# A decoder trunk on eight cores: the first weight block in four transfers with products tile by tile, and retention in chunks of 128 with seven f32 accumulators

## What is computed

```python
q = rotary(rq, pos); k = rotary(rk, pos) * RET_DK**-0.5; v = rv      # 4 heads, 256 wide
def step(S, blk):                                                     # retention, in chunks of C tokens
    s = einsum('bihd,bjhd->bhij', qc, kc) * inner                     # decay mask inside the chunk
    o = einsum('bhij,bjhe->bihe', s, vc) + einsum('bihd,bhde->bihe', qc, S) * q_dec
    S = S * chunk_dec + einsum('bjhd,bjhe->bhde', kc * k_dec, vc)
    return S, o
o = o * rsqrt(mean(o*o) + EPS) * ret_norm_g;  y_ret = (o * silu(rg)) @ w_ret_o
pre = cc * cu;  conv = conv_b + sum(conv_w[t] * xp[:, t:t+L] for t in range(3))
y_conv = (cb * conv * silu(cg)) @ w_conv_o
om = softmax(qm mem_k^T) mem_v * silu(mg);  y_mem = om @ w_mem_o
y = x + (g_ret*y_ret + g_conv*y_conv + g_mem*y_mem) @ w_out;  out = rms_norm(y, final_norm_g)
```

## Time and profile before

| | |
|---|---|
| median of 3 runs | 1253.17 us (1251.75 to 1255.77) |
| the profiled execution | 1262.68 us; its slowest core, core 1, has a span of 1261.1 us |
| spans of the eight cores | 1238.0 to 1261.1 us |
| mean granted TensorE clock | 0.972 to 0.978 on cores 0 to 3, 0.987 to 0.993 on cores 4 to 7 |
| TensorE busy, core 1 | 1190.1 us (94%), 7140 products |
| VectorE, ScalarE, POOL busy | 585.2 us (46%), 461.1 us (37%), 332.6 us (26%) |

### The profile page before, as it was taken

The page is one execution under the profiler, slowest core; times in us unless marked ns, Lnnn a source line. Parts: engine busy times, 40 slices in busy tenths (PEclk is TensorE's granted clock), DMA queues, the critical chain, the costliest instruction groups (busy, mean ns, idle before and its releaser), DMA issues.

```text
span 1261.1 us, 22033 instructions; the slowest of 8 cores (1238.0 to 1261.1 us)
## 1 busy us (share of the span) xinstructions
PE 1190.1 (94%) x7140; PEld 605.1 (48%) x7140; DVE 585.2 (46%) x1058; ACT 461.1 (37%) x1010; POOL 332.6 (26%) x424
## 2 busy tenths in 40 slices
PE   3889999999999999999999999989989799999997
PEld 1444444445554554554444544545545445444443
DVE  3764444442222355556212356556565565322266
ACT  3442233322222444444211254545445346322233
POOL 2332222221000111011333434435334344333300
PEclk9999999999999999999999999989999999999989
DMA  9734111112555686974421033724734633811074
GB/s 219 189 85 67 35 34 35 34 34 39 100 101 101 121 135 114 150 120 82 114 52 34 15 104 128 197 96 137 201 118 145 159 126 106 246 35 34 2 253 164
DMA packets 38000, 134.34 MB, mean 107 GB/s; under 512 B 4736, under 2 KB 8960, under 8 KB 33024
## 3 DMA queue, kind: packets, MB, share of 16 engines
q0 software_dynamic: 10080, 56.63, 27.0%
q1 hardware_dynamic: 27808, 76.30, 18.4%
HBM read 160.56 MB, written 28.98 MB: 150 GB/s over the span
## 4 chain that ended last, share of the span: by engine, by line
PE 75%; DVE 7%; DMA 6%; ACT 5%; issue 4%; SPq 1%; POOL 1%; DVEq 0%; ACTq 0%; POOLq 0%
PE psf L416 73%; DVE tf L1107 3%; DMA pms<-c_maskX 2%; DMA nrp<-arF 2%; DMA arF<-c_cos 1%; PE psh L419 1%; DMA mgd<-xp 1%; ACT th L944 1%; ACT ob L1238 1%; ACT arH L1304 1%; ACT mgd L476 1%; DVE th L953 1%; DVE mgd L485 0%; DVE ssb L940 0%; ACT arH L1164 0%
## 5 line engine op out<-in xcount | busy, mean ns | idle before, releaser
L416 PE MATMUL psf<-hT,w 128*128 128x512 bf16 (+1 forms) x3456 | 694.1, 355 | 3.1 <-ACT hT L499 1.5
L416 PEld LDWEIGHTS psf<-hT,w 128*128 128x128 bf16 x3456 | 315.7, 99 | 336.4 <-issue 44.9
L416 PE MATMUL psf<-ob,w 128*128 128x512 bf16 (+1 forms) x960 | 200.1, 352 | 0.0
L556 ACT ACTIVATE tf<-psf,hbg 128x512 f32<-128x512 f32 (+1 forms) x95 | 60.2, 633 | 210.7 <-PE psf L416 206.7
L416 PEld LDWEIGHTS psf<-ob,w 128*128 128x128 bf16 x960 | 87.8, 99 | 93.5 <-issue 12.0
L416 PE MATMUL psf<-w,hT 128*128 128x512 bf16 (+1 forms) x608 | 130.3, 368 | 1.1 <-ACT th L944 1.1
L567 DVE SCALAR_TENSOR_TENSOR tf<-tf,psf 128x512 f32<-128x512 f32 (+1 forms) x79 | 48.0, 607 | 176.2 <-PE psf L416 168.0
L571 POOL TENSOR_TENSOR mgd<-tf,mgd 128x512 bf16<-128x512 f32 (+1 forms) x79 | 78.8, 1005 | 160.1 <-DVE tf L567 160.1
L1107 DVE TENSOR_TENSOR tf<-psf,arF 128x512 f32<-128x512 f32 (+1 forms) x160 | 95.7, 610 | 29.0 <-POOL arH L1110 7.4
L416 PEld LDWEIGHTS psf<-w,hT 128*128 128x128 bf16 x608 | 59.3, 99 | 59.9 <-issue 6.1
L1110 POOL TENSOR_TENSOR th<-tf 128x512 bf16<-128x512 f32 x32 | 40.7, 1270 | 157.2 <-DVE tf L1107 122.2
(11 more groups left out here) (180 smaller groups left out, 1183.5 us busy)
## 6 DMA issues: line engine op xcount, KB each, us to landing
w<-wb POOLq DMA_DIRECT2D x38, 1024.0 KB, 10.8
mgd<-xp SPq DMA_DIRECT2D x16, 512.0 KB, 11.9
arH<-cmk POOLq DMA_DIRECT2D x12, 512.0 KB, 17.1
arH<-cmv POOLq DMA_DIRECT2D x10, 512.0 KB, 11.8
gaux<-sret SPq DMA_DIRECT2D x8, 512.0 KB, 4.4
xbuf<-sret SPq DMA_DIRECT2D x8, 512.0 KB, 5.1
stgt<-sret SPq DMA_DIRECT2D x8, 512.0 KB, 4.6
hbt<-sret SPq DMA_DIRECT2D x8, 512.0 KB, 5.7
```

The costliest lines, as they stand in the source:

```text
L416: P.op('pe', lambda e: e.matmul(out, lhsT=lhsT, rhs=rhs, start=start, stop=stop), reads=reads, writes=[wbuf])
L556: P.op('act', lambda e, fg=fg, ti=ti, n=n, bcol=bcol: e.activation(out=tf[ti][:, 0:n], in_=psf[fg][:, 0:n], func=AF.Tanh, bias=hbg[:, bcol ...
```

## The change

Four things change together.

1. Start. The first weight block comes in four transfers, one for each product group (the blocks 0 to 7 are packed so that a group's weights lie together), asked for in the order cu, cc, cb, cg from the moment the first token tile is there. Only four token tiles are asked for at first; the next four wait for the third tile's sum. `hT` and the weight slots are tracked in finer pieces. The cu products of group 0 and all four groups of token group 1 are done tile by tile (8 products of 128 columns for each). A dummy activation is put ahead on ScalarE.
2. Conv items. The order of the first items is (0,0), (0,1), (1,0), (1,1), (0,2)... instead of (0,0), (1,0), (0,1)...; the ScalarE operation that starts the convolution is recorded ahead of the cb products, so also ahead of the x_sq in that slot; a small copy goes from POOL to VectorE. The second weight block is asked for later, inside item (0,0).
3. Retention works in chunks of 128 (RC2). Per iteration there are four updates of S instead of two, with four casts instead of two; the scores are four pairs of products of 128 columns, masked by one VectorE operation instead of four; K's four decay copies are one; the outputs need 12 products of 256 columns instead of 14. `tail(i-1)` moves from before the K^T V products to after Q's projection; the two `s_cast` copies move in between the `vg_tile`s; `samp_a` and `samp_b` move earlier in a head's first iteration, and the decode rotation takes four VectorE operations of 256 columns instead of eight of 128. S is sent to memory before Q's projection is recorded, not after the decode part.
4. One of the two bf16 banks becomes a seventh f32 accumulator when retention starts, so one bank is left for transposes.

```diff
-RC2 = 256
+RC2 = 128
+        def wquarter(q, after=()):
+            P.op('pool', lambda e: e.dma_start(out=wsl[0][:].rearrange("p k n -> p (k n)")[:, q * 1024:(q + 1) * 1024],
+                                               in_=wb[0][:, q * 1024:(q + 1) * 1024]),
+                 reads=list(after), writes=[B_w[0][q]], dma_sem='w0q%d' % q)
...
-            x_load()
+            if t == 1:
+                for _ in range(4):
+                    x_load(after=[B_xs[2]])
+            elif t > 1:
+                x_load()
...
+        def tile_mm(f, q, t):
+            c0 = (t % 4) * 128
+            for k in range(8):
+                mm(psf[f][:, c0:c0 + 128], W4[0][:, q, k, :], hT[:, k, t * 128:(t + 1) * 128], k == 0, k == 7, [B_hTt[t], B_w[0][q]], B_psf[f])
...
-                fcb = grp(2, 128)
                 t_cv = tfa()
                 P.op('act', lambda e, t_cv=t_cv, cur=cur, n=n, c=c, v3=v3: e.activation(
                     out=v3(tf[t_cv][:, 0:n]), in_=cur, func=AF.Identity, bias=cbias[:, c:c + 1], scale=cw[:, 2, c:c + 1]),
                     reads=Bp + RC, writes=[B_tf[t_cv]])
+                fcb = grp(2, 1)
...
+        conv_item(0, 0, W0, BW0, 0, 0, slot=slot_a, banks={0: fu0})
+        fb = {q: falloc() for q in (0, 2, 1, 3)}
...
+            for q in (0, 2, 1, 3):
+                tile_mm(fb[q], q, t)
...
+        psf.append(psh[1][:].bitcast(F32)); B_psf.append(B_psh[1])
+        free_h[:] = [0]
+        free_f.append(6)
...
         def kv_state(h, n):
-            cc = n % 2
+            c = n % 4
             fkv = falloc()
             for dch in range(2):
-                for jb in range(2):
-                    c = cc * 2 + jb
-                    mm(psf[fkv][:, dch * 256:dch * 256 + 256], kdt1[:, c, dch * 128:(dch + 1) * 128], vtm1[:, c, :],
-                       jb == 0, jb == 1, [BL_kdt, B_vtm1], B_psf[fkv])
+                mm(psf[fkv][:, dch * 256:dch * 256 + 256], kdt1[:, c, dch * 128:(dch + 1) * 128], vtm1[:, c, :],
+                   True, True, [BL_kdt, B_vtm1], B_psf[fkv])
...
             vg_tile(WB, BWB, g, 0)
+            s_cast(h, g, 0)
             vg_tile(WB, BWB, g, 1)
-            if g == 0 and h > 0:
-                samp_a(h)
+            s_cast(h, g, 1)
+            if g == 0:
+                samp_q(h)
+                samp_b(h)
...
-            r_scores(ki, qi, sx)
-            if i > 0:
-                tail(i - 1)
+            r_scores(ki, qi)
...
-            kv_state(h, 2 * g)
-            kv_cast(h, 2 * g)
-            kv_state(h, 2 * g + 1)
+            for c in range(4):
+                kv_state(h, 4 * g + c)
+                if c < 3 or g == 3:
+                    kv_cast(h, 4 * g + c)
...
+            if i > 0:
+                tail(i - 1)
...
-            fo = [o_chunk(2 * g, qdi, sx), o_chunk(2 * g + 1, qdi, sx)]
-            kv_cast(h, 2 * g + 1)
+            fo = [o_pair(h, g, qdi, 0), o_pair(h, g, qdi, 1)]
+            if g < 3:
+                kv_cast(h, 4 * g + 3)
```

More of the change, by code:

```diff
@@ L242, in _pack_weights @@
         for (name, c0, n, off) in blk:
-            wb[i, :, :, off:off + n] = ws[name][:, c0:c0 + n].reshape(8, 128, n).transpose(1, 0, 2)
+            part = ws[name][:, c0:c0 + n].reshape(8, 128, n).transpose(1, 0, 2)
+            if i < 8:
+                wb[i].reshape(128, 4, 8, 128)[:, off // 128] = part
+            else:
+                wb[i, :, :, off:off + n] = part
     return wb.reshape(len(blocks), 128, 4096)
@@ L283, in build_nc @@
         mgd = sb("mgd", [128, 8, NT], BF16)
-        B_hTg = [[Buf('hTa'), Buf('hTb')] for _ in GROUPS]; B_hT = B_hTg
+        B_hTt = [[Buf('hTa'), Buf('hTb')] for _ in range(NTILE)]
+        B_hTg = [B_hTt[g * 4:min(g * 4 + 4, NTILE)] for g in range(5)]; B_hT = B_hTg
         B_ob = [[Buf('ob') for _ in GROUPS] for _ in range(8)]
@@ L289, in build_nc @@
         wsl = [sb("w%d" % i, [128, 8, 512], BF16) for i in range(NSLOT)]
-        B_w = [Buf('w%d' % i) for i in range(NSLOT)]
+        B_w = [[Buf('w%d' % i) for _ in range(4)] for i in range(NSLOT)]
         gaux = sb("gaux", [128, D])
@@ L463, in build_nc, with x_load @@
         x0 = {'ld': 0, 'n': 0, 'm': 0, 't': 0}
-        def x_load():
+        def x_load(after=()):
             t = x0['ld']
@@ L468, in x_load @@
                 x0['ld'] += 1
-                P.op('sp', lambda e: e.dma_start(out=xr[t % 6], in_=xtile_src(t)), writes=[B_xr[t % 6]], dma_sem='x%d' % (t % 6))
+                P.op('sp', lambda e: e.dma_start(out=xr[t % 6], in_=xtile_src(t)), reads=list(after), writes=[B_xr[t % 6]], dma_sem='x%d' % (t % 6))
         def x_sq():
@@ L705, in conv_item, with slot_a @@
                                                               in_=preS[:, :, 8:10]), reads=Bp, writes=BL_nct)
-        W0, BW0 = wget()
-        W1, BW1 = wget()
+        wstate['issued'] = 1
+        wstate['next'] = 2
+        W0, BW0 = W4[0], B_w[0]
+        W1, BW1 = W4[1], B_w[1]
+        def slot_a(si, post):
+            if post and si == 1:
+                x_sq()
+            elif post and si == 2:
+                x_mul()
+                x_sq()
+                wissue(2)
+        conv_item(0, 0, W0, BW0, 0, 0, slot=slot_a, banks={0: fu0})
+        P.tag = 'conv'
+        fb = {q: falloc() for q in (0, 2, 1, 3)}
+        x_tr()
+        for t in range(4, 8):
+            if t < 7:
+                x_mul()
+                if t < 6:
+                    x_sq()
+                x_tr()
+            for q in (0, 2, 1, 3):
+                tile_mm(fb[q], q, t)
         def x_slot(si, post):
@@ L713, in x_slot @@
             if not post:
-                if x0['t'] < NTILE and x0['t'] < x0['lim']:
+                if x0['t'] < min(NTILE, x0['lim']) and x0['t'] < x0['m']:
                     x_tr()
-            elif x0['m'] < NTILE:
-                x_mul()
+            else:
+                if x0['m'] < x0['n']:
+                    x_mul()
                 if x0['n'] < NTILE:
                     x_sq()
-        for g in range(5):
-            x0['lim'] = 4 * (g + 2)
-            conv_item(0, g, W0, BW0, 0, 0, slot=x_slot)
-            conv_item(1, g, W1, BW1, 1, 1, slot=x_slot)
-            if g == 0:
+        x0['lim'] = 0
+        conv_item(0, 1, W0, BW0, 0, 0, slot=x_slot, banks=fb)
+        for (c, g, lim) in ((1, 0, 10), (1, 1, 12), (0, 2, 14), (1, 2, 16), (0, 3, 17), (1, 3, 17), (0, 4, 17), (1, 4, 17)):
+            x0['lim'] = lim
+            conv_item(c, g, (W0, W1)[c], (BW0, BW1)[c], c, c, slot=x_slot)
+            if (c, g) == (1, 1):
                 wissue(3)
-            if g == 1:
+            if (c, g) == (1, 2):
                 wissue(4)
@@ L1159, in samp_b, with s_cast @@
             ffree(fs)
-        def s_cast(h, s_):
-            for pp in range(2):
-                n = (h * 4 + s_) * 2 + pp
-                P.op('act', lambda e, pp=pp, n=n: e.copy(out=Sqf[:, pp * 1024:(pp + 1) * 1024], in_=pr[n % 4]),
-                     reads=B_pr[n % 4], writes=BL_Sqb[pp * 4:(pp + 1) * 4])
+        def s_cast(h, s_, pp):
+            n = (h * 4 + s_) * 2 + pp
+            P.op('act', lambda e: e.copy(out=Sqf[:, pp * 1024:(pp + 1) * 1024], in_=pr[n % 4]),
+                 reads=B_pr[n % 4], writes=BL_Sqb[pp * 4:(pp + 1) * 4])
         def s_out(h, s_):
@@ L1357, in build_nc @@
             fins = []
+            if g == 0 and h > 0:
+                samp_a(h)
+            P.tag = 'ret'
             qdi = tha()
```

172 lines of the change are left out of this document (92 added, 80 removed).

## The result

The changed kernel takes 1278.51 us (1276.63 to 1281.74, 4 runs) against 1252.78 us (1251.75 to 1255.77): ratio 1.0207 (95%: 1.0184 to 1.0229), slower by 25.7 us. Forecast were 1265 us and a loss of 12. The sign holds, and the time lies inside the wide range (1241 to 1280), but outside the forecast's own (1258 to 1273): the loss is more than twice the one forecast. The profiled execution takes 1281.7 us, its slowest core, core 6, has a span of 1280.2 us.

The account below looks back on a forecast made before the run. TensorE was taken to bound the kernel before, with a serial VectorE and ScalarE chain setting retention's period after. Start -5, retention +7, clock +10 make +12 us: 1265 us median, own range 1258 to 1273, eight in ten 1241 to 1280.

Parts of the forecast that it names:

- The sign: Whole kernel: the change makes it slower, chance 0.6; forecast sum +12 us.
- The ring: Retention, inner iterations: serial chain through VectorE, ScalarE and K^T V closes at 22.1 us, 2.1 more than 19.98.
- 4.5 + 1.9 - 1.0: Retention, ScalarE from first V tile's Silu to last V copy: two decode casts added, decay copies joined, given as 5.25 us.
- The transfer of S: Retention, change of head: S asked for some 9 us earlier, so its wait is gone; otherwise 9 us stay.
- The mechanism of the clock: Retention: short TensorE waits of 0.35, 1.35 and 0.85 us close together, 15 times, bring the granted clock down.
- The start: First products and conv items: earlier products and less idle time give -5 us, ends -9 and +2.
- the conv items lose their idle time of 7.3 us to 1.5 to 2: Conv stretch: x_sq's new place in ScalarE's queue removes TensorE waits, -5.5 us.
- The clock: Retention: eight falls of the granted clock at about 1.2 us each, +10 us, ends 0 and +20.
- The change of head: Retention, a head's first iteration: 25.3 us (24.4 to 26.1); three changes of head give 13 us back.
- So the bank does not help: Retention, output pairs: the seventh accumulator brings nothing, because Q's rotation comes 3 us later.
- the ring and heads: Retention, 12 inner iterations of 22.1 us and three of 25.3 us: 341.1 against 334.2 us, +7 us.
- All of it goes wrong: Rival: clock falls every iteration (+20), start gives nothing (tile 3 late, second weight block waited for): +27, 1280 us, chance 0.15.

Follow-up runs that it names:

- the run with extra products: Changed kernel plus 15 unread products of 256 columns per iteration, 10 ahead of the first output pair and 5 ahead of the second: 1268.19 us, ratio 1.0171.
- The mended start: Kernel before with the new start; sums and scalings of tiles 4 to 8, tile 4's transposes and the second weight block's request earlier: 1240.13 us, ratio 0.9940.
- the run without both: Changed kernel, decode mask asked for one iteration earlier, decode transposes at a change of head in an f32 accumulator: 1277.84 us, ratio 1.0239.
- the first of the last two versions: Changed kernel with two buffers for S, earlier decode mask, head-change decode transposes in an f32 accumulator, sums and scalings of tiles 4 to 8 earlier: 1219.28 us, ratio 0.9784.

## Why the prediction was too small

What held. The ring: its period of 22.1 us is in the trace of the changed kernel wherever the clock holds inside a head, and in every inner iteration of the run with extra products. So do its members: updates 0.81 to 0.82 us behind a cast, TensorE's waits of 1.33, 0.23, 1.09 and 0.56 us against 1.3, 0.35, 1.35 and 0.85. (One term is added up too short: 4.5 + 1.9 - 1.0 is 5.4 us, not 5.25; the trace has 5.1.) The transfer of S is no longer waited for. The mechanism of the clock is the one named, from the earlier trace rows: a cluster of short waits. So the sign is not luck.

What failed, with its size:

- *The start, -5 us, measured 0.* The first tiles came some 2 us earlier than forecast (the first cu products at 16.4 us instead of 18.6, the last done at 27 instead of 28.8), since tile 3's sum began at 14.7 us, the early end of what I had allowed. The step that failed is "the conv items lose their idle time of 7.3 us to 1.5 to 2". I looked at x_sq's place in a conv item, not at the seam: tile 5's sum stands in the cb slot of item (0,0), behind that item's own chain, and its x_mul takes 2.66 us instead of 1.28. TensorE waits 3.66 us, then works at a clock of 0.55 to 0.60 for some 6 us. In the conv stretch of 76 us it is still idle for 6.6 us, and not for 1.5 to 2. The mended start shows that the gain was there to be had.
- *The clock, +10 us as eight falls of 1.2; measured about ten of 1.7.* On core 6 the clock falls ten times between the first and the last mask: in six of the eight later intervals inside a head, at each of the three changes of head, and in the first interval: +17 us. I had counted only K's first products as slow; the second output pair is slow as well. The eight falls were too few and their price too low.
- *The change of head, 25.3 us.* The pair of iterations was forecast at 25.3 + 22.1 = 47.4 us and is 28.1 + 20.9 = 49.0 even with the clock up (the shortest on any core; on core 6 one is 30.2 at full clock, with the wait for the mask): 5 us over three heads. With the falls the pairs are as long as in the kernel before, so the 13 us that the changes of head were to give back did not come. I had summed VectorE's extra work and left out the single bank for transposes and the decode mask, a transfer that the change asks for 6 us before its use; the one pair without a fall in the run without both is 47.8 us, so they are 1.2 of the 1.6 us.
- *"So the bank does not help"* was wrong; without it the loss is 3.3%.

With these: the ring and heads 7 + 5, the clock 17, the start 0 make +29 against the 27 that retention shows and 25.7 in the medians. This is close to the rival "All of it goes wrong" (+27, 1280 us, chance 0.15): the falls came in most iterations and the start gave nothing, though by the seam and not by a late tile 3, and no wait for the second weight block is in the changed kernel's rows.

## To carry to other kernels

When a state is updated more often, first ask whether its copy and its next update fight for one buffer: here 3 x 0.82 us on a serial chain decided between 2% slower and 0.5% faster. Here three waits of TensorE within 3.1 us cost 1.7 us more than their sum of 1.88 us in most iterations, since the work behind them ran at the lower clock; end the cause of such a cluster first, and then count idle time. After a wait is removed look at the next reader on the same engine; of single waits taken away at the change of head none gave anything in the changed kernel; with the chain shortened by two buffers for S, mask and bank together gave 11 us.

## What was not expected of the hardware

A wait of 1.32 us once per iteration, with one of 0.35 us near the outputs, leaves the granted clock at 0.99 to 1.00 over retention (two buffers for S alone, and the first of the last two versions), while 0.23, 1.09 and 0.56 us within 3.1 us bring it to 0.82 and 0.75 in two slices of 4 us. The same cluster does so in six of eight intervals inside a head on core 6 and not in the other two; why it spares some is not shown. Filling the wait of 1.32 us changes nothing. Products of no use, 16 of 256 columns in each iteration, made the kernel 4 to 7 us faster. A scaling of 1024 columns on VectorE took 2.66 us instead of 1.28 while POOL worked beside it (L723 in the rows of the start); elsewhere in both kernels it takes 2.2 us beside the same POOL operation. No run shows that POOL is the cause.
